# Sums of squares and the gate projection of a hybrid recurrent trunk as float32r passes over high parts and remainders

## What is computed

```python
# gated DeltaNet, each of 8 heads of 128 channels
q = _l2norm(q) * DN_DK ** -0.5            # x * rsqrt(sum(x*x) + eps), over the head's channels
k = _l2norm(k)
o_dn = _rmsnorm(o_dn, w['dn_norm'][j]) * jax.nn.silu(z_dn)
# GLA, each of 4 heads of 256 channels
o_gla = _rmsnorm(o_gla, w['gla_norm'][j]) * jax.nn.silu(z_gla)
# SSD, 4 groups of 256 channels
y_ssd = _rmsnorm(y * jax.nn.silu(z), w['ssd_norm'][j])
# after the mixer of either layer
gate = jax.nn.sigmoid(_rmsnorm(h, w['ple_norm'][li]) @ w['ple_w_gate'][li])
h = h + gate * (p[li] @ w['ple_w_proj'][li])   # p: 544 x 256, w_proj: 256 x 2048
```

## Time and profile before

| | before |
|---|---|
| median of three runs | 2507.78 us (2507.23 to 2509.1) |
| profiled execution: span | 2502.7 us; its own time is not listed |
| TensorE busy | 2426.0 us, 97% of the span |
| VectorE busy | 1254.3 us, 50% |
| ScalarE busy | 951.4 us, 38% |
| GpSimd busy | 367.3 us, 15% |
| dense slices in the chain that ended last | 71% of the span |
| DMA | 271.30 MB, mean 108 GB/s |

### The profile page before, as it was taken

How to read it: one execution, slowest core, us unless ns; L and a number is a source line. 1 busy time by engine, 2 the same in 40 slices (tenths; PEclk the granted TensorE clock), 3 DMA queues, 4 the chain that set the end, 5 groups by cost and what they waited for, 6 DMA issues and landing times.

```text
span 2502.7 us, 52615 instructions
## 1 busy us (share of the span) xinstructions
PE 2426.0 (97%) x22783; PEld 2298.4 (92%) x22783; DVE 1254.3 (50%) x2301; ACT 951.4 (38%) x1531; POOL 367.3 (15%) x558
## 2 busy tenths in 40 slices
PE   7999999999999999999999999999999999999996
PEld 7998889888889999989999999988899999999996
DVE  6644655545544554732253456466656562243332
ACT  5423444234433343432252243244445552243222
POOL 3101101110100010111111111122212121111111
PEclk9999999999999999999999999999999999999998
DMA  9333333333343543653233333233323354323232
GB/s 244 98 103 98 110 96 107 88 96 97 114 118 96 157 142 94 202 172 89 85 99 99 109 99 100 73 91 87 84 80 107 90 162 148 87 83 94 77 87 74
DMA packets 375543, 271.30 MB, mean 108 GB/s; under 512 B 24419, under 2 KB 346733, under 8 KB 374800
## 3 DMA queue, kind: packets, MB, share of 16 engines
q1 hardware_dynamic: 341424, 172.53, 25.5%
q0 software_dynamic: 22080, 72.77, 9.0%
q10 hardware_dynamic: 11808, 22.63, 2.6%
HBM read 220.24 MB, written 48.37 MB: 107 GB/s over the span
## 4 chain that ended last, share of the span: by engine, by line
PE 88%; DVE 4%; ACT 4%; DMA 2%; issue 2%; SPq 0%; ACTq 0%; POOL 0%; DVEq 0%; POOLq 0%
PE psd L570 71%; PE psw L593 2%; PE psw L592 2%; PE psw L620 1%; PE psw L670 1%; PE psw L648 1%; DVE arena L1965 1%; DMA w_raw<-in_ab_w_in_dram 1%; PE psw L656 1%; PE psw L642 1%; DMA mix<-in_x_prompt_dram 1%; ACT w_hi L1137 1%; PE psw L662 0%; PE psw L634 0%; PE psw L970 0%
## 5 line engine op out<-in xcount | busy, mean ns | idle before, releaser
L570 PE MATMUL psd<-xh,w_hi 128*128 128x272 f32 x5056 | 1107.0, 300 | 15.7 <-DVE xl L1741 6.5
L570 PE MATMUL psd<-xh,w_lo 128*128 128x272 f32 x5056 | 1048.5, 289 | 0.4 <-issue 0.4
L570 PE MATMUL psd<-xl,w_hi 128*128 128x272 f32 x5056 | 1046.2, 288 | 0.0
L570 PEld LDWEIGHTS psd<-xh,w_hi 128*128 128x128 f32 x5056 | 797.4, 189 | 71.0 <-issue 37.9
L570 PEld LDWEIGHTS psd<-xl,w_hi 128*128 128x128 f32 x5056 | 797.2, 189 | 0.0
L570 PEld LDWEIGHTS psd<-xh,w_lo 128*128 128x128 f32 x5056 | 793.2, 189 | 0.0
L1681 DVE TENSOR_TENSOR w_lo<-w_raw,w_hi 128x512 fp32r<-128x512 f32 x632 | 434.5, 705 | 403.4 <-ACT w_hi L1137 402.0
L1137 ACT CAST w_hi<-w_raw 128x512 fp32r<-128x512 f32 x632 | 377.2, 615 | 576.6 <-PE psd L570 513.6
L2560 POOL TENSOR_TENSOR states<-states,extra 128x544 f32<-128x544 f32 x59 | 80.0, 1355 | 524.6 <-ACT extra L1192 524.6
L2366 DVE TENSOR_TENSOR extra<-psd,rstd 128x544 f32<-128x544 f32 x32 | 23.2, 724 | 156.3 <-PE psd L570 139.2
L2345 DVE TENSOR_TENSOR arena<-arena,psd 128x544 f32<-128x544 f32 x32 | 23.0, 720 | 133.5 <-PE psd L570 127.1
(11 more groups left out here) (513 smaller groups left out, 2377.9 us busy)
## 6 DMA issues: line engine op xcount, KB each, us to landing
w_raw<-in_ab_w_in_dram SPq DMA_DIRECT2D x224, 256.0 KB, 3.0
w_raw<-in_cd_w_in_dram SPq DMA_DIRECT2D x148, 256.0 KB, 3.0
w_raw<-in_ple_w_gate_dram SPq DMA_DIRECT2D x128, 256.0 KB, 3.1
w_raw<-in_ab_w_out_dram SPq DMA_DIRECT2D x64, 256.0 KB, 2.9
w_raw<-in_cd_w_out_dram SPq DMA_DIRECT2D x64, 256.0 KB, 3.0
uT_scratch<-mix ACTq DMA_DIRECT2D x53, 272.0 KB, 2.4
hT_scratch<-arena POOLq DMA_DIRECT2D x8, 1088.0 KB, 5.6
arena<-hT_scratch POOLq DMA_DIRECT2D x8, 1088.0 KB, 9.3
```

What stands on the lines that cost most here:

```text
L570: mm = pe.matmul(out[:, D0 + HALF * half:D0 + HALF * (half + 1)], w[:, r, k % QH, :], x[:, k, HALF * half:HALF * (half + 1)], start=(k == ...
```

## The change

It does four things. The three DeltaNet sums (`ssq`, `ssk`, `n`) become two float32r passes each: ScalarE copies the squares to float32r (`high`), VectorE subtracts these from the squares in place (`low`), and TensorE adds the pass over the high parts and the pass over the remainders (`summed`). In GLA and SSD VectorE first adds the two squares and TensorE makes one fp32 pass of the sum. The gate projection becomes six float32r passes a tile, with high parts and remainders of p (made once a layer) and of w_proj (made for every tile, `proj_hi` on ScalarE and `proj_lo` on VectorE, one tile ahead). And three set-up semaphores are folded into others. `arenaR`, `rawsR` and `mixR` are float32r views of the memory of `arena`, `raws` and `mix`.

```diff
-            once(("gate", layer), f"p{i}", "in_copied")
+            add(("gate", layer), f"p{i}", "p_lo", (KT + 2) * layer + i + 1)
...
-PARAM_DMAS = len(PARAM_ROWS) + 6
+PARAM_DMAS = len(PARAM_ROWS) + 7
...
-        arena = sb("arena", [P, KT * T])
+        with nc.sbuf_tensor("arena", [P, KT * T], F32) as arena:
+            pass
+        arenaR = sb("arenaR", [P, KT * T], F32R)
...
+        def high(i, n=1):
+
+            return arenaR[:, T * (12 + i):T * (12 + i + n)]
+
+        def low(i, n=1):
+            return arenaR[:, T * i:T * (i + n)]
...
+        p_hi = rawsR[:, 1280:1280 + 2 * T].rearrange("p (k t) -> p k t", k=2)
+        p_lo = rawsR[:, 0:2 * T].rearrange("p (k t) -> p k t", k=2)
+        wp = raws[:, 2368:2880].rearrange("p (s k n) -> p s k n", s=2, k=2)
+        wp_hi, wp_lo = (mixR[:, 512 * i:512 * i + 512].rearrange("p (s k n) -> p s k n", s=2, k=2)
+                        for i in range(2))
...
+            def summed(W, hi, lo):
+
+                all_tokens(W, ones[:, :].bitcast(F32R), hi, start=True, stop=False)
+                return all_tokens(W, ones[:, :].bitcast(F32R), lo, start=False, stop=True)
...
                 W = group(u, "ssq")
-                pe.wait_ge(S["dn_sq"], h + 1)
-                all_tokens(W, ones[:, :], slot(6), start=True, stop=True).then_inc(S["work_ready"], 1)
+                pe.wait_ge(S["dn_hi"], 2 * h + 1)
+                pe.wait_ge(S["dn_lo"], 2 * h + 1)
+                summed(W, high(0), low(6)).then_inc(S["work_ready"], 1)
                 W = group(u, "ssk")
-                all_tokens(W, ones[:, :], slot(7), start=True, stop=True).then_inc(S["work_ready"], 1)
+                summed(W, high(1), low(7)).then_inc(S["work_ready"], 1)
...
                 W = group(u, "n")
-                pe.wait_ge(S["dn_osq"], h + 1)
-                all_tokens(W, ones[:, :], osq, start=True, stop=True).then_inc(S["work_ready"], 1)
+                pe.wait_ge(S["dn_hi"], 2 * h + 2)
+                pe.wait_ge(S["dn_lo"], 2 * h + 2)
+                summed(W, high(0), low(4)).then_inc(S["work_ready"], 1)
...
-                pe.wait_ge(S["gl_osq"], 2 * h + 2)
-                for e in range(2):
-                    mm = all_tokens(W, ones[:, :], slot(9 + e), start=e == 0, stop=e == 1)
-                mm.then_inc(S["work_ready"], 1)
+                pe.wait_ge(S["pair_sum"], h + 1)
+                all_tokens(W, ones[:, :], slot(9), start=True, stop=True).then_inc(S["work_ready"], 1)
...
-                    pe.wait_ge(S["sp_sq"], p + 1)
-                    for e in range(2):
-                        mm = all_tokens(W, ones[:, :], stage[:, e, :], start=e == 0, stop=e == 1)
-                    mm.then_inc(S["work_ready"], 1)
+                    pe.wait_ge(S["pair_sum"], GLA_H + p // 2 + 1)
+                    all_tokens(W, ones[:, :], stage[:, 0, :], start=True, stop=True).then_inc(S["work_ready"], 1)
...
-                    pe.wait_ge(S[f"wp_loaded{c % 2}"], 16 * (8 * layer + c // 2 + 1))
+                    pe.wait_ge(S["p_hi"], (KT + 2) * layer + c + 3)
+                    pe.wait_ge(S["p_lo"], (KT + 2) * layer + c + 3)
                     for k in range(2):
-                        mm = all_tokens(W, wp[:, c % 2, k, :], pT[:, k, :], start=k == 0, stop=k == 1)
+                        for i, (w, x) in enumerate(((wp_hi, p_hi), (wp_hi, p_lo), (wp_lo, p_hi))):
+                            mm = all_tokens(W, w[:, c % 2, k, :], x[:, k, :], start=k + i == 0, stop=k == 1 and i == 2)
                     mm.then_inc(S["work_ready"], 1)
...
-                act.activation(slot(0, 3), slot(0, 3), ACT.Silu).then_inc(S["dn_silu"], 1)
-                act.wait_ge(S["dn_silu"], h + 1)
-                act.activation(slot(6, 2), slot(0, 2), ACT.Square).then_inc(S["dn_sq"], 1)
+                link(act.activation(slot(0, 3), slot(0, 3), ACT.Silu))
+                link(act.activation(slot(6, 2), slot(0, 2), ACT.Square))
+                act.copy(high(0, 2), slot(6, 2)).then_inc(S["dn_hi"], 1)
...
                 act.activation(slot(4), W[:, 0:T], ACT.Square).then_inc(S["dn_osq"], 1)
+                act.wait_ge(S["dn_osq"], h + 1)
+                act.copy(high(0), slot(4)).then_inc(S["dn_hi"], 1)
                 W = group(u, "n")
...
+            def proj_hi(layer, c):
+
+                if c == KT:
+                    return
+                act.wait_ge(S[f"wp_loaded{c % 2}"], 16 * (8 * layer + c // 2 + 1))
+                if c >= 2:
+                    act.wait_ge(S["work_ready"], NO[("gate", layer), f"g{c - 2}"] + 1)
+                act.copy(wp_hi[:, c % 2], wp[:, c % 2]).then_inc(S["p_hi"], 1)
...
-                    act.copy(pT[:, i, :], W[:, 0:T]).then_inc(S["in_copied"], 1)
+                    act.copy(p_hi[:, i, :], W[:, 0:T]).then_inc(S["p_hi"], 1)
+                proj_hi(layer, 0)
...
                     sigmoid(layer, c)
+                    proj_hi(layer, c + 1)
...
+                dve.wait_ge(S["dn_hi"], 2 * h + 1)
+                dve.tensor_tensor(low(6, 2), slot(6, 2), high(0, 2).bitcast(F32), ALU.subtract).then_inc(S["dn_lo"], 1)
                 for n in ("ssq", "ssk", "gbc"):
                     skip(u, n)
                 dve.wait_ge(S["dn_rs"], h + 1)
...
+                dve.wait_ge(S["dn_hi"], 2 * h + 2)
+                dve.tensor_tensor(low(4), slot(4), high(0).bitcast(F32), ALU.subtract).then_inc(S["dn_lo"], 1)
                 skip(u, "n")
                 dve.wait_ge(S["dn_rstd"], h + 1)
...
+                dve.tensor_tensor(slot(9), slot(9), slot(10), ALU.add).then_inc(S["pair_sum"], 1)
                 if h + 1 < GLA_H:
                     gates(u, "lgn", h + 1)
...
                 if e2:
+                    dve.wait_ge(S["sp_sq"], p + 1)
+                    dve.tensor_tensor(stage[:, 0, :], stage[:, 0, :], stage[:, 1, :], ALU.add).then_inc(S["pair_sum"], 1)
                     skip(u, "n")
...
+            def proj_lo(layer, c):
+
+                dve.wait_ge(S["p_hi"], (KT + 2) * layer + c + 3)
+                dve.tensor_tensor(wp_lo[:, c % 2], wp[:, c % 2], wp_hi[:, c % 2].bitcast(F32), ALU.subtract)\
+                   .then_inc(S["p_lo"], 1)
...
+                    if c == 0:
+                        group(u, "p1")
+                        for i in range(2):
+                            dve.wait_ge(S["p_hi"], (KT + 2) * layer + i + 1)
+                            dve.tensor_tensor(p_lo[:, i, :], psw[NO[u, f"p{i}"] % 2][:, 0:T], p_hi[:, i, :].bitcast(F32),
+                                              ALU.subtract).then_inc(S["p_lo"], 1)
+                        proj_lo(layer, 0)
                     W = group(u, f"g{c}")
                     dve.wait_ge(S["gate_sig"], KT * layer + c + 1)
                     dve.tensor_tensor(e, e, W[:, WT], ALU.mult).then_inc(S["gate_read"], 1)
                     dve.wait_ge(S["gate_read"], KT * layer + c + 1)
                     dve.tensor_tensor(hT(c), hT(c), e, ALU.add).then_inc(S["gate_done"], 1)
+                    if c + 1 < KT:
+                        proj_lo(layer, c + 1)
                     if layer:
...
-            pool.dma_start(cb16[:, :], I["cb"]).then_inc(S["masks_loaded"], 16)
+            pool.dma_start(cb16[:, :], I["cb"]).then_inc(S["params_loaded"], 16)
...
                         pool.wait_ge(S["gate_read"], KT * layer + c - 1)
+                        pool.wait_ge(S["p_lo"], (KT + 2) * layer + c + 1)
```

More of the change, by code:

```diff
@@ L191 @@
 bc_conv bc_silu bc_b bc_cb
-sp_conv sp_silu sp_D sp_ebc sp_A sp_v sp_um sp_s sp_gs sp_snew sp_i sp_o sp_y sp_sq sp_ln sp_rstd sp_out
+sp_conv sp_silu sp_D sp_ebc sp_A sp_v sp_um sp_s sp_gs sp_snew sp_i sp_o sp_y sp_sq pair_sum sp_ln sp_rstd sp_out
 lr_conv lr_r lr_i lr_a lr_t lr_sq lr_hs lr_y
-tail_copied tail_made sp_sel ssd_stored y_stored0 y_stored1 p_loaded wp_loaded0 wp_loaded1 gate_sig gate_read gate_done out_copied tok_rstd out_dve out_act out_smp zeroed consts_set masks_loaded""".split()
+tail_copied tail_made sp_sel ssd_stored y_stored0 y_stored1 p_loaded p_hi p_lo wp_loaded0 wp_loaded1 gate_sig gate_read gate_done out_copied tok_rstd out_dve out_act out_smp""".split()
 PARAM_ROWS = {
@@ L233, in trunk @@
         w_hi, w_lo = sb("w_hi", [P, NW, QH, P], F32R), sb("w_lo", [P, NW, QH, P], F32R)
-        raws = sb("raws", [P, 6 * T])
-        mix = sb("mix", [P, 5 * T])
+        with nc.sbuf_tensor("raws", [P, 6 * T], F32) as raws:
+            pass
+        rawsR = sb("rawsR", [P, 6 * T], F32R)
+        with nc.sbuf_tensor("mix", [P, 5 * T], F32) as mix:
+            pass
+        mixR = sb("mixR", [P, 5 * T], F32R)
         stage = mix[:, 3 * T:5 * T].rearrange("p (e t) -> p e t", e=2)
@@ L1050, in _ @@
             pe.wait_ge(S["consts_loaded"], 16)
-            pe.wait_ge(S["consts_set"], 1)
+            pe.wait_ge(S["dve_chain"], 1)
             for t in range(NT + 1):
@@ L1083, in _ @@
             mm.then_inc(S["work_ready"], 1)
-            pe.wait_ge(S["masks_loaded"], 16)
+            pe.wait_ge(S["params_loaded"], PARAM_DMAS * 16)
```

(10 more changed lines are left out.)

10 lines of the change are left out of this document (3 added, 7 removed).

## The result

The changed kernel takes **2517.0 us** (median of 7 runs, 2511.91 to 2522.85), the kernel before 2507.46 us (7 runs, the three known ones among them, 2504.65 to 2510.8). The ratio is 1.0037, 95% interval 1.0025 to 1.0048: 9.3 us slower, 6 to 12. Forecast were +6.4 us and 2514 us.

A forecast was written before the change was run, and what follows sets the result against it. TensorE, busy 97% of the span, was taken to bound the kernel. DeltaNet +17, GLA -3.7, SSD -1.0, gate projection -10.9 gave +1.4; the clock added +5: 2507.8 + 6.4 = 2514 us, range 2500 to 2524.

The forecast's parts named there:

- Passages without a drop: DeltaNet, from one head to the next: seven passages lengthen by 0.9 to 3.2 us, 16.5 together, before clock effects.
- the store and the second cast wait for VectorE: 430.5: DeltaNet, into head 4: ScalarE's store and second weight cast wait for VectorE's eviction ending at 430.0, until 430.5.
- The clock: Granted clock falls after four in ten of some eleven long DeltaNet waits: 6.6 us less 1.5 already paid, +5 us.
- GLA: Four heads: one fp32 pass of two gone, 0.92 each, VectorE's add hidden; -3.7 us.
- SSD: Four pairs: one pass saved, 0.92, but the unhidden add loses 0.7; -0.25 a pair, -1.0 us.
- The gate projection: Two layers of 16 tiles: 0.34 saved each, new high and low parts covered by slices; -10.9 us.
- C: Rival at DeltaNet's ssq: new copies and subtractions are covered; 2489 us, or 2479 with norm sums and SSD covered; chance 0.08.
- D: Rival: ssk-to-dm chain shifts only by TensorE's own, DeltaNet passages cost nothing; -15.6 + 0.5, 2493 us; chance 0.07.
- A: Rival: the clock never falls on these DeltaNet waits; +1.4 - 1.5, 2508 us, no change; chance 0.17.
- B: Rival: the clock falls at nearly every long DeltaNet wait; +1.4 + 15, 2523 us; chance 0.13.
- E: Rival: GpSimd port exclusion holds DeltaNet's seven long subtractions 0.68 us each; passages cost 4.8 more, 2519 us; chance 0.05.
- The lower end of the long subtraction: DeltaNet's 1088-column VectorE subtraction at 1.2 us instead of 1.29; lower ends of copy and subtraction were said to give +15.

The follow-up runs named there:

- experiment 3: Changed kernel plus float32r matmuls nobody reads, filling TensorE's waits at ssq of heads 1 to 7; 2517.14 us, ratio 1.0031 to the kernel before.
- experiment 1: Only the DeltaNet part of the change; GLA, SSD and gate stage as in the kernel before; 2529.55 us, ratio 1.0081 to it.
- experiments 4: Changed kernel with VectorE evicting the finished tile before, not after, its wait and subtraction at ssq; 2507.32 us, ratio 0.9995 to the kernel before.
- 7 to 10: Changed kernel with more slices ahead of ssq, 2520.53 us; with norm sum n as before, 2510.38; with all DeltaNet sums as before and early eviction, 2490.54; then 10.
- 10: All parts but DeltaNet's, early eviction, one slice of each DeltaNet head moved ahead of dm; 2486.4 us, ratio 0.9914 to the kernel before.
- 12: Changed kernel with early eviction, long copy and subtraction in halves, one slice per DeltaNet head moved ahead of dm; 2498.2 us, ratio 0.9966 to the kernel before.
- experiment 5: Changed kernel with DeltaNet squares written as float32r and summed in one pass, no remainders, copies or subtractions; 2498.3 us, ratio 0.9955 to the kernel before.

## Why the prediction came out

**Durations.** The new operations took what the rows of equal width said: long copy 1.10 (1.11 taken), long subtraction 1.29 (1.29), short ones 0.65 and 0.72. The pass at 0.25 us held: in n the second one starts at 428.95 and the next slice at 429.20.

**The waits and passages.** TensorE waited 0.73 at n (0.9 forecast; 1.3 into head 7) and 1.84 to 2.60 at ssq (1.9 to 2.7). Head 4's ssq was to start at 429.35 in the time of before; it did at 438.81 - 9.37 = 429.44, and the eviction ended at 429.93 (430.0 forecast). Head 0 waits 0.97 at ssq, where I had no wait, and its o comes out at +0.1; that says little, since the start of the program alone moves this place by more (ledgers above). Passages without a drop are right within 0.1 us into heads 1, 2, 5, 6 and 7 (for 1 and 2 by the row of experiment 3; the one into 6 has a drop that cost nothing). Into 3 and 4 they are 0.6 too short, 1.2 in all. That step, "the store and the second cast wait for VectorE: 430.5", priced the cast and not the store: between the eviction's end (439.30) and the cast (439.75) ScalarE first issues the DMA.

**The clock.** Forecast were eleven long waits with 4 in 10 dropping, +5 us. There were eleven of 1.67 us or more, and seven drops; but that the number agrees is luck. Seven are at ssq and three at dm; at dm of head 6 TensorE waited 0.63, and the eleventh is the one at t1 of head 7, which was there before (1.76, without a drop). The steps that failed are the share of waits with a drop, four in ten where this execution had seven of eleven, and the one price of 1.5 for all: it holds behind dm (three drops, and the one at t1, less the one of before: +4.5), while the three at ssq cost 0.5, 1.0 and nothing. Together +6.0: too few drops at too high a price, two errors that nearly cancel. Other executions draw other drops, so neither share is a rule.

**DeltaNet's sum.** Passages 16.5 + 0.5 for the last n + 1.2 (stores) + 6.0 (clock) = 24.2; TensorE's waits with "issue" as releaser are 1.75 us in this stretch where they were 0.75, +1.0: 25.2 of the 25.5 measured in the profile, for 22 forecast. The times give 20.3 for the part alone. The difference is that of single executions and medians (experiment 1); the forecast of 22 lies between. What the "issue" waits are was not studied.

**GLA** gave back 0.9 a head, 3.6 (3.7 forecast); its gates wait less instead, against 2.93 of the earlier trace rows:

```profile
834.30 0.78 DVE L2109 TENSOR_SCALAR arena<-psw,pv 128x544 f32<-128x544 f32 x1 [2.29 <-ACT arena L1347]
```

**SSD** gave 0.15 a sum, 0.6 in all (0.25, 1.0 forecast). TensorE waits 0.75 for the add where it waited for nothing. The mechanism was right; the part left over was smaller than forecast.

```profile
1671.74 0.67 PE L611 MATMUL psw<-mix,ones 128*128 128x256 f32 x2 [0.75 <-DVE mix L2299]
```

**The gate projection** was covered and gave 0.34 a tile, as forecast; one tile's group now lasts from 2485.93 to 2487.44, 1.51 us:

```profile
2485.93 0.28 PE L611 MATMUL psw<-rawsR,mixR 128*128 128x256 f32 x1
...
2487.44 0.72 PE L1039 MATMUL psw<-ones,states 128*128 128x1 f32 x6
```

The 1.4 us lost in the second stage's first tile are a drop of the clock (0.74 in 2285:2290). It isn't the change's: experiment 1, with the gate stage of before, lost 1.5 there, and experiments 4, 7 to 10 and 12, with the changed one, lost nothing.

**The rivals.** C and D (covered sums) needed a readiness at TensorE's arrival; from head 1 on it came 1.8 us or more after. A (no drops) and B (nearly all) fail by the count: seven of eleven. E (long subtractions held up by GpSimd) did not happen: L1983 has a mean of 1292 ns over its 8 calls.

**A slip in the sum.** The lower end of the long subtraction, 1.2 for 1.29 us in seven passages, gives +16.4 for DeltaNet and not the +15 stated. The forecast doesn't use it.

## What to carry to other kernels

Before cheapening an engine's work, follow the chain behind it to the next point where it must wait anyway: here TensorE's time ahead of dm was worth nothing (14 us of cheaper passes gave 3, experiment 5), and what the cheaper form put on ScalarE was paid in full. When an instruction that waits is put at the head of a queue, look first at what stood there: moving one eviction ahead of it gave back 10.5 us, 7.9 of them in the passages. And a wait that can't be shortened is a place for independent work: one slice of each head moved ahead of dm was worth 5.3 and 6.5 us (experiments 10 and 12).
